# A hybrid attention and SwiGLU layer: where ScalarE's copies and roundings stand in an attention step, and when a round's score operands are made

## The reference

```
h    = rms_norm(x, norm_mix);  proj = h @ w_in + b_in
o_a  = 16 heads (group A), each: compressed-block branch, selected-block branch,
       window branch, mixed by sigmoid gates; 4 K/V heads per branch
o_b  = 16 heads (group B): causal window of 128 with a sink per head; 2 K/V heads
x    = x + concat(o_a, o_b) @ w_out
h    = rms_norm(x, norm_ffn)
x    = x + (silu(h @ w_gate) * (h @ w_up)) @ w_down;   out = rms_norm(x, norm_final)
```

## Time and profile before

| | |
|---|---|
| median of 3 runs | 2263.94 us (2262.27 to 2265.55) |
| profiled execution | 2263.91 us |
| its span, first to last instruction | 2262.2 us |
| busy: TensorE, VectorE, ScalarE, GpSimd | 2202.3, 969.7, 711.4, 146.8 us |
| mean granted TensorE clock | 0.987 of full |
| lowest slices of the clock (1/40 of the span each) | 0.8 and 0.7, between 566 and 679 us |
| chain that ended last, by engine | PE 93%, ACT 4%, DVE 1%, issue 1%, DMA 1% |

### The profile page before, as it was taken

The page is one execution under the profiler, slowest core; times in us unless marked ns, Lnnn a source line. Parts: engine busy times, 40 slices in busy tenths (PEclk is TensorE's granted clock), DMA queues, the critical chain, the costliest instruction groups (busy, mean ns, idle before and its releaser), DMA issues.

```text
span 2262.2 us, 25273 instructions
## 1 busy us (share of the span) xinstructions
PE 2202.3 (97%) x10231; PEld 1801.4 (80%) x10231; DVE 969.7 (43%) x1622; ACT 711.4 (31%) x1076; POOL 146.8 (6%) x116
## 2 busy tenths in 40 slices
PE   8999999998699999999999999999999999999998
PEld 6888777775478888888888888888888888888887
DVE  6623766767734343333423323332333233342253
ACT  5222555656723262212222221212222122222233
POOL 3000112111100000000000000000000000000000
PEclk9999999998799999999999999999999999999999
DMA  8770212211232223322223222232222322233221
GB/s 317 219 212 28 66 52 66 59 49 59 91 130 93 93 94 99 106 93 93 93 100 104 93 93 93 98 105 93 93 93 97 107 93 93 93 97 107 94 93 75
DMA packets 126453, 227.72 MB, mean 101 GB/s; under 512 B 6384, under 2 KB 28976, under 8 KB 126256
## 3 DMA queue, kind: packets, MB, share of 16 engines
q1 hardware_dynamic: 124048, 222.58, 30.2%
q10 hardware_dynamic: 2336, 4.20, 0.5%
HBM read 207.89 MB, written 18.87 MB: 100 GB/s over the span
## 4 chain that ended last, share of the span: by engine, by line
PE 93%; ACT 4%; DVE 1%; issue 1%; DMA 1%; DVEq 0%; ACTq 0%
PE bank L1487 25%; PE bank L1489 25%; PE bank L1488 25%; PE bank L1756 2%; PE bank L1760 2%; PE bank L1758 2%; PE bank L1853 2%; PE bank L1727 2%; PE bank L1653 2%; PE bank L1685 1%; ACT proj_kv L820 1%; DMA work<-bias_scratch 1%; PE bank L1538 1%; ACT raw L843 0%; ACT prob_x L820 0%
## 5 line engine op out<-in xcount | busy, mean ns | idle before, releaser
L985 DVE TENSOR_TENSOR w_lo<-raw,w_hi 128x2048 fp32r<-128x2048 f32 x160 | 366.8, 2292 | 1073.8 <-ACT w_hi L702 1073.7
L1487 PE MATMUL bank<-act_lo,w_hi 128*128 128x512 f32 x1920 | 749.8, 391 | 1.0 <-DVE w_lo L985 0.5
L1488 PE MATMUL bank<-act_hi,w_lo 128*128 128x512 f32 x1920 | 747.2, 389 | 0.0
L1489 PE MATMUL bank<-act_hi,w_hi 128*128 128x512 f32 x1920 | 747.2, 389 | 0.0
L702 ACT ACTIVATE w_hi<-raw 128x2048 fp32r<-128x2048 f32 x160 | 306.7, 1917 | 1167.7 <-PE bank L1489 1161.2
L1487 PEld LDWEIGHTS bank<-act_lo,w_hi 128*128 128x128 f32 x1920 | 360.7, 188 | 77.2 <-issue 2.5
L1488 PEld LDWEIGHTS bank<-act_hi,w_lo 128*128 128x128 f32 x1920 | 360.6, 188 | 75.2 <-issue 0.8
L1489 PEld LDWEIGHTS bank<-act_hi,w_hi 128*128 128x128 f32 x1920 | 360.5, 188 | 75.1
L1489 PE MATMUL bank<-ff_hi,w_hi 128*128 128x512 f32 x656 | 255.2, 389 | 0.0
L1487 PE MATMUL bank<-ff_lo,w_hi 128*128 128x512 f32 x656 | 255.2, 389 | 0.0
L1488 PE MATMUL bank<-ff_hi,w_lo 128*128 128x512 f32 x656 | 255.2, 389 | 0.0
(11 more groups left out here) (195 smaller groups left out, 1619.9 us busy)
## 6 DMA issues: line engine op xcount, KB each, us to landing
raw<-in_w_gate SPq DMA_DIRECT2D x44, 1024.0 KB, 5.1
raw<-in_w_up SPq DMA_DIRECT2D x44, 1024.0 KB, 5.1
raw<-in_w_down SPq DMA_DIRECT2D x44, 1024.0 KB, 5.0
raw<-in_w_in SPq DMA_DIRECT2D x16, 1024.0 KB, 11.1
raw<-in_w_out SPq DMA_DIRECT2D x16, 1024.0 KB, 5.1
mini_raw<-in_w_in SPq DMA_DIRECT2D x56, 256.0 KB, 2.9
bias_scratch<-prob_x SPq DMA_DIRECT2D x32, 320.0 KB, 7.5
proj_kv<-in_x SPq DMA_DIRECT2D x4, 1024.0 KB, 8.8
```

Source lines behind the costliest of these rows:

```text
L985: nc.vector.tensor_tensor(w_lo[:, step % RING, 0:n], raw[:, step % RAW, 0:n], w_hi[:, step % RING, 0:n].bitcast(F32), ALU.subtract)\
L1487: nc.tensor.matmul(dst[c][:, :], wh[:, t, cs], x_lo(t), start=start, stop=False)
L1488: nc.tensor.matmul(dst[c][:, :], wl[:, t, cs], x_hi(t), start=False, stop=False)
L1489: done = nc.tensor.matmul(dst[c][:, :], wh[:, t, cs], x_hi(t), start=False, stop=stop)
```

## The change

ScalarE's step gets a new order: the copies of x-2, the bias of a finished run, the roundings of step x+1's pieces and a part of the stack come ahead of the exps of x. VectorE's step has the pieces' corrections and its part of the stack directly behind `normalise`, ahead of `copy_third`. The stack of round r is made in three parts in the steps `first_item(r) - 3`, `- 2` and `- 1`: 3, 3 and 2 roundings and corrections of 8 in group A, 2, 2 and 2 of 6 in group B. Round 0's stack is made as before. TensorE, GpSimd and SP have the same order as before.

```
-STACK_AT = [None] + [first_item(r - 1) + 2 for r in range(1, ROUNDS)]
+STACK_PARTS = 3
+STACK_STEP = {first_item(r) - STACK_PARTS + part: (r, part) for r in range(1, ROUNDS)
+              for part in range(STACK_PARTS)}
...
+        def stack_part(r, part):
+            count = len(stack_sources(r)[0])
+            if part is None:
+                return 0, count
+            per = -(-count // STACK_PARTS)
+            return per * part, min(count, per * (part + 1))
...
 ScalarE:
             for x in range(N_ITEMS + 3):
+                if 2 <= x <= N_ITEMS + 1:
+                    copies(x - 2)
+                for run in runs_ended(x - 1):
+                    mini_bias(run)
+                for m in minis_of(x + 1):
+                    mini_hi_of(m)
+                if x in STACK_STEP:
+                    stack_hi_of(*STACK_STEP[x])
                 if x < N_ITEMS:
                     exps(x)
-                    if x in STACK_AT:
-                        stack_hi_of(STACK_AT.index(x))
                 if x == SPLIT_AT:
...
-                if 2 <= x <= N_ITEMS + 1:
-                    copies(x - 2)
                 (out_hi, out_a_hi as before)
-                for run in runs_ended(x - 1):
-                    mini_bias(run)
-                for m in minis_of(x + 1):
-                    mini_hi_of(m)
...
 VectorE:
                     normalise(x - 1)
+                for m in minis_of(x + 1):
+                    mini_lo_of(m)
+                if x in STACK_STEP:
+                    stack_lo_of(*STACK_STEP[x])
                 (copy_third, copy_v as before)
-                if x in STACK_AT:
-                    stack_lo_of(STACK_AT.index(x))
                 (split_lo, out_lo, out_a_lo as before)
-                for m in minis_of(x + 1):
-                    mini_lo_of(m)
```

More of the change, by code:

```diff
@@ L754, in add_bias, with stack_hi_of @@
                       .then_inc(biased, 1)
-            def stack_hi_of(r):
-                if r >= 2:
+            def stack_hi_of(r, part=None):
+                first, last = stack_part(r, part)
+                if r >= 2 and first == 0:
                     act.wait_ge(scored, 4 * first_item(r - 1))
                     act.wait_ge(mini_biased, 2 * r if 4 * r >= NSA_HEADS else 2 * r - 2)
-                else:
+                elif first == 0:
                     act.wait_ge(biased, ALL_READ)
-                for n, (src, dst, scale) in enumerate(stack_sources(r)[0]):
+                for n in range(first, last):
+                    src, dst, scale = stack_sources(r)[0][n]
                     if r == 0 and n in (3, 6):
@@ L1188, in copy_v, with stack_lo_of @@
                 nc.vector.tensor_copy(tile_of(t), bank[:, :]).then_inc(v_copied, 1)
-            def stack_lo_of(r):
-                if r >= 2:
+            def stack_lo_of(r, part=None):
+                first, last = stack_part(r, part)
+                if r >= 2 and first == 0:
                     dve.wait_ge(scored, 4 * first_item(r - 1))
                 for k, (n, src, hi, dst, scale) in enumerate(stack_sources(r)[1]):
+                    if not first < n <= last:
+                        continue
                     if r == 0 and k in (4, 7):
```

## The result

| | before | after |
|---|---|---|
| median of 5 runs | 2263.94 us (2262.07 to 2265.65) | 2286.81 us (2278.64 to 2287.72) |
| profiled execution | 2263.91 us | 2286.81 us |
| its span | 2262.2 us | 2285.1 us |
| mean granted TensorE clock | 0.987 | 0.981 |

The changed kernel takes 1.009 times the time of the one before, interval 1.0074 to 1.0107: 22.9 us more, where I forecast 1.2 less. It is slower, outside the range of 2255 to 2270.

The account below looks back on a forecast made before the run. TensorE was taken to bound the first 40 steps, the triangle VectorE, ScalarE, TensorE the last 16. -6.1 + 0.6 + 2.5 + 3.0 - 1.2 = -1.2 us against 2263.9 gave 2262.7 us, range 2255 to 2270.

Parts of the forecast that it names:

- Waits that leave in A: Steps 0 to 39: TensorE's short waits in steps 2, 8 and 32 go, -6.1 us.
- A: Steps 0 to 39, bound by TensorE: -6.1 us for waits that go, +0.6 for waits the edit adds.
- The third L1061 wait: Step 2: this 1.1 us wait stays, since the second piece there still waits for TensorE.
- What the same edit adds in steps 9, 19 and 29: Last corrections made just before a round's first score: +0.2 us a round, +0.6 in all.
- My own sign of being wrong: Forecast wrong if steps 9, 19, 29 each wait over 1 us, or VectorE idles under 4 us from step 41 to the load.
- The passage: Step 39 into group B: step 40's score 3.0 us late behind the last correction; +2.5 us, bounds +0.2 to +3.0.
- B: Steps 41 to 51, up to round 7's last correction: 61.3 us instead of 58.3, +3.0, bounds -4.8 and +7.
- The table behind the big load: Step 53's mask stays 15.1 us behind the last correction, its table queued behind the 4 MB residual load; delays aren't hidden.
- Tail: Steps 53 to 57: earlier copies bring output rounding and step 55's mask and exps forward; -1.2 us, bounds -2.4 and 0.
- Operands at the last moment: Rival: each round's first score waits for VectorE's last corrections; +9.1 us, 2273.0; chance 0.20.
- The loop opens: Rival: TensorE's waits on transposes' copies go, and VectorE's idle time with them; -12.1 us, 2251.8; chance 0.20.
- The waits before step 40 only move: Rival: no gain in steps 0 to 39, the rest as forecast; +4.3 to +4.9 us, 2268.5; chance 0.10.

Follow-up runs that it names:

- e9: Changed kernel with the tables of heads 29 to 31 issued ahead of the residual's load: 2273.67 us, 1.0045 of the kernel before.
- e1: Changed kernel with the third copy again ahead of the pieces' corrections and the stack part on VectorE: 2276.14 us, 1.0066 of the kernel before.
- e6: Changed kernel with three parts only in rounds 4 to 7, rounds 1 to 3 made in one lump: 2268.54 us, 1.0022 of the kernel before.
- e4: Changed kernel with each of the three parts made one step earlier: 2259.96 us, 0.9980 of the kernel before.
- e7: Changed kernel with the parts one step earlier and the third copy first on VectorE: 2251.45 us, 0.9948 of the kernel before.

## Why the prediction was wrong

**Waits that leave in A: right, undersized.** I had -6.1. The score of step 5 starts 4.6 us earlier (the lump of step 2 and its piece, for which I had 2.7: step 3 loses its 2.7 us of idle time, and its matmuls, which before ran at a granted clock of 0.84, run at 1.00 and take 1.9 less), that of step 9 5.4 earlier, and step 33 gives 2.9 where I had 2.5: -8.3. The third L1061 wait stays, as forecast.

**What the same edit adds in steps 9, 19 and 29: this step failed.** I took +0.2 a round, +0.6; it is +6.2 a round, +18.6. My own sign of being wrong, a wait over 1 us in steps 9, 19 and 29, came true. I had followed one chain, from the last correction to the next score, and put its end 7.8 us after step 9's score. In e9, at full clock, it ends 10.8 us after it, 1.97 of them the third copy's; without these I estimate 8.9, so this chain was short by 1.1, and L1649 waits 0.6 us. I had not followed the third copy, which the diff visibly moves behind `mini_lo_of` and `stack_lo_of` and which frees the bank of TensorE's next transposes. Its 1.97 us, with the score's 0.55, make step 9's wait; and the pieces behind these transposes make the later roundings late. e9's trace has the same two waits with the clock at 1.00 and gives their price alone: steps 9 and 10 take 18.98 us against 15.94, +3.0. The other 3.2 us a round are the clock, on which I had counted only in the passage and in B, and which is in part chance (last section). e1 shows the copy to be the holder of the first wait, and shows as well that its place alone doesn't do: the wait moves to the score.

**The passage: the mechanism right, the size just over its bound.** +2.5 forecast, bounds 0.2 to 3.0; +3.4 measured (10.3 at step 39, 13.7 at step 41). The score of step 40 waits 3.86 us for the last correction and comes 3.0 us late against step 39's, as worked out; the step behind it is 0.5 us longer than before.
What I had drawn on of the Trainium skill (TensorE: Matmul & The Clock Gate, section "Architectural detail: the array is 16x 32x32, not 1x 128x128", on strictly first in, first out queues) the trace bears out: the exps never pass what is written ahead of them, and in step 42 they stand behind copies that wait 3.84 us for products.

**B: the mechanism right, the size not.** +3.0 forecast with bounds -4.8 and +7, +8.7 measured. VectorE's work was forecast as 53.5 us and is 53.51; its idle time was taken as 7.8 and is 13.5, over the bound of 12. I had put waits of about 2 us on step 41, 0.4 on step 42, half a us on others and 1.3 to 3 on the output roundings of steps 44 and 48; the first scores wait up to 8.42 us, 24.8 in the four rounds, and of VectorE's 13.5 us idle 8.9 (3.7 + 5.2) stand ahead of the corrections of output roundings, 5.4 (3.2 + 2.2) before. One part I had not seen at all: step 42's copies wait for all of group A's products (3.84 us), and the exps are now behind them. e6 puts the price of the parts of rounds 4 to 7, the passage included, at 9.0 us against the same order with lumps.

**The table behind the big load: right.** Step 53's mask stays 14.8 us behind the load (15.1 before), and VectorE's 7.13 us of wait for the table hide nothing of what was lost ahead of the load, since the load itself comes later. The table of shifts and e9 show it.
That the table waits for the whole load agrees with the rule that I had named (the Trainium skill, DMA: Bandwidth & Descriptors, section "Queues, rings and completion order"): 14.33 us in this queue, against 2.3 alone.

**Tail:** -1.2 forecast, +0.5 measured: from the load to the first output unit 33.82 us against 33.37. That is outside my bounds of -2.4 and 0. The gain came and was lost again. Counted from step 53's mask, step 55's mask comes 1.2 us earlier (10.30 against 11.50), as forecast, and the transposes of step 56 start 2.3 us earlier (12.62 against 14.97). But from there to the first output unit the same matmuls, busy throughout in both kernels, take 6.43 us at a granted clock of 0.50 against 3.32 at 1.00. I had left the clock out of this term. No experiment was made on it alone, so whether it falls there each time stays open.

**The rivals.** "Operands at the last moment" (0.20) came nearest; its condition, that a round's last L1197 ends later than TensorE's work of the step before, is what e4 and e7 take away. But before step 40 its wait is the smaller one (0.55 us, the third copy's 1.97), and the third copy it doesn't name. At 2273.0 it was undersized by 13.8 us, 12.6 of them its 2 us a round for 6.2 in A. "The loop opens" (0.20) held in its first half: the waits on copies left, but VectorE's idle time did not, because another wait at the same place took over. e7, without that wait, comes to the time that this rival gave, 2251.45 measured and 2251.8 forecast: A with -6.1 and B with -4.6 are as it had them (-6.1, -4.8), but that the totals agree is partly luck, with -2.7 in the passage where it had 0 and -0.5 in the tail where it had -1.2. "The waits before step 40 only move" (0.10) didn't hold: of the waits for L1061 only the 1.1 us of step 2 are left.

Added up: -8.3 + 18.6 + 3.4 + 8.7 + 0.5 = +22.9 us.

## What to carry to other kernels

When work is cut up and spread up to its deadline, try to have every part ready a whole step before its reader. In the last step each wait on the way comes back to the engine that waits for the result: here that one step was worth 26.9 us, and the same split one step earlier, with the buffer-freeing copy first, was some 12 us better than the kernel before. For each instruction that a diff moves something ahead of, ask which buffer it frees and who writes there next: a copy of 0.42 us, moved behind five corrections, held TensorE for up to 2 us each time. And where a small load that is needed soon stands in a queue behind a large one that isn't, try them in the other order: it was worth 7 us here, in two kernels.

## What the runs showed of the hardware that I had not expected

**The same waits with and without a fall of the clock.** The kernel after and e9 have the same instructions and the same order up to step 39. Steps 9 and 10 of e9, then steps 19 and 29:

```profile
303.83:314.70 10.87, 8.31 (x44) 6.65 (x42) 8.17 (x22) 8.22 (x22) 1.72 (x1) 1.00 0.33 92
314.70:322.81 8.11, 8.11 (x54) 6.15 (x54) 4.43 (x14) 2.73 (x8) 1.72 (x1) 1.00 0.15 41
379.50:390.23 10.73, 8.32 (x44) 6.65 (x42) 8.06 (x22) 8.10 (x22) 1.72 (x1) 1.00 0.31 90
454.61:467.06 12.45, 9.93 (x45) 7.83 (x43) 8.18 (x22) 8.21 (x22) 1.72 (x1) 0.86 0.28 82
```

With L1701 waiting 1.97 us in both, step 9 took 12.46 us at clock 0.86 in the one execution and 10.87 at 1.00 in the other; in e9 the clock fell in round 3 alone (step 29, 12.45 us). A fall costs 3.2 us over the two steps ((12.46 + 9.70) - (10.87 + 8.11)). After a wait of 2 us in dense work the clock sometimes falls to its low level, then, and sometimes not. From step 1's score to step 39's e9 needs 282.26 us, 6.3 less than the kernel after and only 1.8 more than e4: how much the early parts gain in A depends on whether the clock falls. Three such rounds with and without would make 9.5 us, and the kernel after has the widest runs of all, 2278.64 to 2287.72, where the kernel before spreads over 3.6; that these are the same thing is likely but not shown, since there is no trace of the 2278.64 run.

**"Issue" as the name of a real wait.** 7.9 us of waits named "issue" at L1701 were waits for another engine's copy: they went to 0.3 when the copy was moved, and the copy's end stood 0.1 us ahead of each of the four long ones' start. A wait of that name that is longer than a few tenths is worth a look at what the other engines finish just then.
